# Values behind scores: a block of TensorE work placed earlier in the slots of three attention mixers

## What is computed

```
s = q . k * scale (+ bias or mask)            # over latent and context keys
p = softmax(s)[..., :n_keys]
o = p . v
out = concat(o over heads) @ w_o
```

## Time and profile before

| | of the span |
|---|---|
| TensorE matmul (PE) | 2900.1 us, 99%, 17613 instructions |
| TensorE weight load (PEld) | 2810.0 us, 96% |
| VectorE (DVE) | 2274.4 us, 78% |
| ScalarE (ACT) | 1252.3 us, 43% |
| GpSimd (POOL) | 166.6 us, 6% |
| granted TensorE clock | 1.000 |
| HBM | 485.33 MB read, 167 GB/s |

### The profile page before, as it was taken

One profiled execution on the slowest core, in us unless ns is written; L12 is line 12 of the kernel. 1 busy time (PEld: TensorE's weight loads), 2 busy tenths in 40 slices (PEclk: granted clock), 3 DMA queues, 4 the chain that ended last, 5 costly groups with the idle time before them and its releaser, 6 DMA issues.

```text
span 2931.5 us, 44455 instructions
## 1 busy us (share of the span) xinstructions
PE 2900.1 (99%) x17613; PEld 2810.0 (96%) x17613; DVE 2274.4 (78%) x3459; ACT 1252.3 (43%) x2001; POOL 166.6 (6%) x171
## 2 busy tenths in 40 slices
PE   8999999999999999999999999999999999999999
PEld 6999979999999998999999997899999999989999
DVE  6889887888787877888788777778888887777653
ACT  3332464443333266443333348644333333664432
POOL 0000220000000030000000012000000001320000
PEclk9999999999999999999999999999999999999999
DMA  7555314555455512455455531255555555324342
GB/s 290 208 211 216 145 42 170 187 201 204 181 190 190 217 56 93 186 193 210 180 191 199 198 120 46 73 201 193 199 190 192 193 207 195 108 75 173 128 143 93
DMA packets 87722, 490.22 MB, mean 167 GB/s; under 512 B 11824, under 2 KB 13168, under 8 KB 51376
## 3 DMA queue, kind: packets, MB, share of 16 engines
q1 hardware_dynamic: 83696, 480.42, 44.4%
q0 software_dynamic: 3904, 8.24, 1.1%
HBM read 485.33 MB, written 3.29 MB: 167 GB/s over the span
## 4 chain that ended last, share of the span: by engine, by line
PE 55%; issue 38%; DVE 4%; ACT 1%; DMA 1%; POOL 1%; SPq 0%; DVEq 0%; POOLq 0%; ACTq 0%
PE ps L840 16%; PE ps L859 8%; PE ps L845 8%; PE ps L880 5%; PE ps L1060 4%; PE ps L863 4%; PE ps L824 1%; PE ps L995 1%; PE ps L1035 1%; DMA boot<-in_mod_w 1%; PE ps L1134 1%; PE ps L976 1%; PE ps L980 1%; DVE tmp L1685 0%; PE ps L1079 0%
## 5 line engine op out<-in xcount | busy, mean ns | idle before, releaser
L840 PE MATMUL ps<-h_hi,w_hi 128*128 128x386 f32 x2688 | 908.2, 338 | 0.0
L840 PE MATMUL ps<-h_lo,w_hi 128*128 128x386 f32 x2688 | 893.4, 332 | 0.0
L1593 DVE TENSOR_TENSOR w_lo<-w_raw,w_hi 128x2048 fp32r<-128x2048 f32 (+3 forms) x282 | 706.9, 2507 | 30.0 <-ACT w_hi L1263 29.6
L1613 DVE CUSTOM_DVE_ANT_0 F_junk<-F_slab,cond,mod_b 128x1024 f32<-128x1024 f32 x544 | 707.2, 1300 | 12.7
L1263 ACT ACTIVATE w_hi<-w_raw 128x2048 fp32r<-128x2048 f32 (+4 forms) x278 | 578.7, 2082 | 14.8 <-DMA w_raw<-in_ffn_dn 10.8
L840 PEld LDWEIGHTS ps<-h_lo,w_hi 128*128 128x128 f32 x2688 | 512.5, 191 | 0.0
L840 PEld LDWEIGHTS ps<-h_hi,w_hi 128*128 128x128 f32 x2688 | 503.1, 187 | 0.4 <-ACT w_hi L1263 0.4
L845 PE MATMUL ps<-h_hi,w_lo 128*128 128x386 f32 x2688 | 494.4, 335 | 0.0
L859 PE MATMUL ps<-F_act_hi,w_hi 128*128 128x384 f32 x1408 | 473.6, 336 | 0.0
L859 PE MATMUL ps<-F_act_lo,w_hi 128*128 128x384 f32 x1408 | 473.3, 336 | 0.0
L845 PEld LDWEIGHTS ps<-h_hi,w_lo 128*128 128x128 f32 x2688 | 469.0, 187 | 0.0
(11 more groups left out here) (371 smaller groups left out, 3465.9 us busy)
## 6 DMA issues: line engine op xcount, KB each, us to landing
w_raw<-in_ffn_gu SPq DMA_DIRECT2D x176, 1024.0 KB, 4.8
F_slab<-in_mod_w SPq DMA_DIRECT2D x272, 512.0 KB, 5.6
w_raw<-in_ffn_dn SPq DMA_DIRECT2D x64, 1408.0 KB, 6.4
w_raw<-in_d_w SPq DMA_DIRECT2D x8, 1536.0 KB, 6.7
boot<-in_mod_w SPq DMA_DIRECT2D x8, 1024.0 KB, 10.2
w_raw<-in_a_w SPq DMA_DIRECT2D x4, 1536.0 KB, 6.6
w_raw<-in_b_w SPq DMA_DIRECT2D x4, 1536.0 KB, 6.7
w_raw<-in_c_w SPq DMA_DIRECT2D x8, 544.0 KB, 3.6
```

Source lines behind the costliest of these rows:

```text
L840: pe.matmul(ps[:, 2 * par + u, 0:N_MOVE], w[0][:, k, u, :], h[:, k, :], start=(k == 0 and h is h_hi), stop=False)
L1593: dve.tensor_tensor(w_lo[par][:, 0:w], w_raw[par][:, 0:w], w_hi[par][:, 0:w], ALU.subtract).then_inc(w_split_lo.sem, 1)
L1613: dve.tensor_tensor_reduce(out=junk[:], in0=w, in1=cond[:, c, :], scale=scale, scalar=mod_b[:, n:n + 1], op0=ALU.mult, op1=ALU.add, accum_ ...
```

## The change

In mixers A, B and D `values(b - 3)` stands directly behind `scores(b)`, ahead of the first outputs, of `hold_clock`, of `turn_p` and of the early projections. In slots 16, 17 and 18, which have no scores, it is the first work of the slot. C keeps its order. No instruction is added or removed, and no other engine's queue changes. Every wait stays with its call.

```diff
                     first, last = ahead(kind, b)
                     if b < BATCHES:
                         scores(s, b)
+                    if kind != "C" and b >= 3:
+                        values(s, b - 3, "cl")
                     for m, p in first:
                         output(s, m, p)
                     if kind == "A" and b == BATCHES - 5:
...
                             values(s, b - 3, "c")
                         turn_qk(s, (b + 1) // 2, "k")
                     else:
-                        if b >= 3:
+                        if kind == "C" and b >= 3:
                             values(s, b - 3, "cl")
                         if turn:
                             turn_qk(s, (b + 1) // 2, "qk")
```

## The result

The median of four executions is 2963.37 us (2963.20 to 2964.88), against 2933.64 us (2933.39 to 2933.72) for the kernel before: ratio 1.0103, 95% interval 1.009 to 1.0115. The change costs 29.7 us, 1.0%. The forecast was 2960 us.

A forecast was written before the change was run, and what follows sets the result against it. TensorE's queue bounds filled slots; VectorE's order and the path between engines bound empty ones. A 9.5, B 9.2 and D 7.9 make 26.6 us, on 2931.5 gives 2958.1, plus 2.1 around the span: 2960 us, range 2944 to 2970.

The forecast's parts named there:

- Part 4: Slots without projections: loops wait for o_lo, then copies; A +2.9, +1.4, B +1.6, +1.5, D +1.3; ends +2.2, +3.2, +3.0.
- Part 2: Odd filled slots: turn_qk waits uncovered for ScalarE's probability copies, 0.87 us more each; D 3.6 us with the even slots' gains.
- Part 1: Even filled slots: nothing waits, and 48 projection matmuls run unbroken, a gain of 0.18 us per slot.
- the ends: Last slots of the mixers' loops: waits for copies, o_hi and o_lo add 3.2 us in B, 2.2 in A, 3.0 in D.
- Part 3: Slot 7 of A and B: late o_lo delays values, then turn_qk waits for copies; +3.0 and +2.9 counting from slot 3.
- the joins: Scores to values, not in the trace: 0.2 us assumed, 0 to 0.4 as ends, 4 us either way over 19 filled slots.
- Rival 2: A's slot 11: TensorE idles and the clock falls to 1.2 GHz, +6 to +12 us on the forecast, 2969 us; chance 0.12.
- Rival 1: Only the copy wait bites, o_lo being early enough: D 3.6, A and B 1.3 each, 2942 us; chance 0.14.
- Rival 3: Faster: joins count, waits don't, and values fill idle time; at most 7.3 us, 2926.3 us; chance 0.05.
- Rival 4: It evens out: gains meet the filled slots' losses and loops stay with VectorE, 2934 to 2938 us; chance 0.07.
- The signs that the forecast named: Waits led by turn_qk, then values for o_lo; turn_p's gone; D's projections in 48s; A, B, D longer by 9.5, 9.2, 7.9.
- the three signs of being wrong: turn_qk under 1.5 us behind turn_p, no wait for o_lo in slot 7, or a clock other than 1.00.

The follow-up runs named there:

- run 1: Kernel before with values directly behind scores only in D's odd slots 3 to 11: 2937.56 us against 2933.57.
- run 2: Values early only in D's odd slots 3 to 11, with the late projection piece cut in two around the query/key transposes: 2932.93 us, ratio 0.9998.
- run 3: Kernel before with values directly behind scores only in D's even slots 4, 6, 8 and 10: 2936.06 us, ratio 1.0009.
- run 8: Changed kernel with o_hi directly behind p_copy on ScalarE in slots 4 and 6 of A and B: 2961.01 us, ratio 1.0094.
- run 9: Changed kernel; in A's and B's slots 8 to 16 o_hi goes ahead of p_copy, o_lo between maximum and inverse: 2953.85 us, ratio 1.007.
- run 11: Values early in A/B slots 3, 4, 8 onward and D except 4, 6, 8, 10; o_lo earlier in A/B, hold_clock ahead, projections cut: 2937.68 us, ratio 1.0015.
- run 6: Changed kernel with the 14 clock-holding matmuls of A's slot 11 moved ahead of values: 2960.03 us, ratio 1.009.
- after: The changed kernel itself, with values directly behind scores in A, B and D: 2963.37 us, ratio 1.0103 to the kernel before.
- run 7: Kernel before without the 14 clock-holding matmuls of A's slot 11: median 2934.71 us, four executions at 2933.35 to 2933.62, six at 2934.66 to 2936.24.

## Why the prediction was right, point by point

The time was 3.4 us above the forecast, on a loss of 29.7. By place, in us, from the traces: A and B from one even slot's maximum on VectorE to the next, D from scores to scores, an end as what is left of its mixer (slots 8 to 10 had no term in the sum; in part 4 they were argued to be nothing):

| | forecast | measured |
|---|---|---|
| A: up to slot 8 | 3.0 | 3.38 |
| A: 8 to 10 | 0 | 0.06 |
| A: 10 to 12, with the holding block | 2.9 | 4.39 |
| A: 12 to 14 | 1.4 | 1.39 |
| A: end | 2.2 | 1.63 |
| B: up to slot 8 | 2.9 | 3.20 |
| B: 8 to 10 | 0 | 0.58 |
| B: 10 to 12, 12 to 14 | 1.6, 1.5 | 1.53, 1.28 |
| B: end | 3.2 | 2.58 |
| D: filled slots | 3.6 | 6.69 |
| D: 12 to 14 | 1.3 | 1.54 |
| D: end | 3.0 | 1.62 |
| sum | 26.6 | 29.87 |

**Part 2, the copy wait, was right** in kind and nearly in size: 0.80 us for each of D's five slots (run 1) against 0.87. Run 2 shows the cause, since work under the copies removes it.

**Part 1, even filled slots, had the wrong sign.** The step that failed is "Nothing waits" with its gain of 0.18 us from an unbroken block. The block of 48 in the earlier trace rows was taken from slot 2, whose two pieces go to two PSUM banks. From D's slot 4 on both pieces go to bank 7, and the second has to wait until ScalarE has copied the first one out. In the kernel before, values stood between the two pieces and hid that copy. The forecast named values as cover for p_copy and did not ask what else it covered. Cost: 0.62 us a slot (run 3) in place of -0.18, in D 3.2 us over four slots. That is as much as the whole error of the sum, 3.3 us, because the other errors cancel: 1.5 us for the clock and 0.6 for B's slots 8 to 10 on one side, 2.6 for the ends on the other. The same wait shows in A and B, 0.25 us in slot 5 and 0.58 in slot 6.

The Trainium skill, "PSUM — Partial Sum Buffer", section "PSUM bank collisions raise a hardware error", says that a write by TensorE into a bank that another engine reads at the same time is an error. By that rule this wait can be covered, or avoided with another bank, but not dropped; no run here tried what happens without it.

**Part 3, slot 7, was right** in its sum and in its chain: 3.38 and 3.20 against 3.0 and 2.9, and turn_qk of A's slot 7 at 394.98 us against 394.56. Run 8 bears out the chain through o_hi for 1.1 us in A and 0.8 in B. The way there was not as forecast. From scores to scores A's slots 3 to 7 cost +0.77, -0.21, +0.60, +0.66 and +1.70 us; for slots 5 and 6 the forecast had about 0 and -0.18. In slot 5 stand 0.16 us of wait for o_lo and 0.25 for the raw copy, which delay all behind them: o_lo of slot 7 ended at 392.15 us instead of 391.71. Slot 6's wait of 0.58 us behind the raw copy delays only the late piece and the next scores, and slot 7 waits for o_lo that much less: 0.81 us in A and 0.71 in B, where 1.5 to 2 was forecast. A chain that goes by when o_lo is ready forgives such errors.

**Part 4, the loops, was right** where it used rows alone: 1.53, 1.28 and 1.39 against 1.6, 1.5 and 1.4. Run 9 shows that o_lo's place in VectorE's queue makes some 8 to 9.5 us of the loss of A and B. Runs 9 and 11 show that the copies alone cost little in the loops of A and B, 0.2 to 0.3 us over three loops (with the clock-holding block off the path). For B's slots 8 to 10 nothing was forecast, and they cost 0.58 us. What was argued without a row each, the ends, came out high by 2.6 us in sum (5.8 against 8.4). The number of 2960 is good in part by luck, because this and the missed raw copies and clock cancel. Two smaller slips: the wait of D's values for o_lo shows twice in the kernel before, 0.31 us in slot 13 beside the 0.86 in slot 15, and not once; and the spreads that the forecast names, 4 us for the joins and half of the 8 us argued without a row, give 2952 as the lower end of its own range and not 2949.

**Rival 2, the clock, half came true.** It fell at the place named and after the wait named. Its price did not hold: one stretch of some 3.4 us at half clock, which costs 1.4 to 1.6 us, instead of 6 to 12; the next loop, 1.39 us over, ran at full clock. The forecast's own 2.9 us for this loop was short by that 1.5. It had also put the block itself on the path, 1.7 us, and run 6 bears that out.

**Rival 1**, the copy wait alone, falls by run 9: moving o_hi and o_lo, with the copy waits as they were, takes 9.5 us off. **Rival 3**, joins as a gain, has the right sign and 0.13 us a slot (run 2). **Rival 4** falls with the loops.

**The signs that the forecast named** came out mixed. turn_qk waits 0.7 to 0.8 us in every odd slot from 3 to 13 but slot 5 of A and B, the waits of turn_p are gone, B is longer by 9.17 us against 9.2 and C is unchanged. But the list is led by o_lo and not by the copies, the empty slots wait 1.0 to 1.5 us for it (2.7 in A's slot 11) and not 1.5 to 3, D's blocks of 48 are broken by the raw-copy wait, and A and D are longer by 10.85 and 9.85 us against 9.5 and 7.9. Of the three signs of being wrong one came: the clock wasn't 1.00 throughout. It cost too little to matter for the number.

## What to carry to other kernels

Before a block is moved ahead, list every transfer that it covers at its old place: here p_copy, and the raw copy between two writes to one bank; each can become a wait of its own length. Where other idle time already stands in the loop, the new wait may take its place and cost almost nothing, so compare the loop's length and not the sum of the waits (run 11). A block that has a wait of its own should not stand ahead of work that doesn't need it: in a queue that is worked in order, one late input (o_lo) then holds the transposes, their copies and the next scores. When a price is taken from a row, check that the row has the same banks and neighbours as the case, not just the same instructions.

## What the runs showed of the hardware that was not expected

An idle stretch of TensorE of the same length was followed by half clock in one profiled execution and not in another. After 2.72 us of idle time it was at 0.50 (after), after 2.71 us it stayed at 1.00 (run 8), and after 2.99 us it fell in the profiled execution of run 7, whose ten executions lie in two groups 1 us and more apart. In both falls TensorE was at work again before the clock went down, by an estimate from the mean clocks of the stretches 0.75 us after the wait had ended in after (0.99 from 415 to 416 us) and 0.45 in run 7 (0.92 from 410 to 412). A fall costs 1.4 to 1.6 us where short blocks are on the path. With 14 matmuls of 128x128 inside the stretch (1.83 us, run 6) the clock stayed at 1.00 in the profiled execution, and the executions lay within 0.32 us.

The Trainium skill, "TensorE: Matmul & The Clock Gate", Part 1, says that the unit that watches TensorE's activity runs freely and isn't started by the kernel. By that rule, whether a stretch of idle time counts depends on where it falls, and the two groups agree with it; no run here shows the unit itself.
